# Output projection of a streaming encoder step: a block's tokens as 512 + 36 columns in place of 274 + 274

## What is computed

```python
h = rmsnorm(x, g1)
z = h @ w_in                                  # 1024 -> 8 token mixers' inputs and 3 x 1024 gates
ya, yb, yc = mlstm(z), short_conv(z), diff_attention(z)      # each (tokens, 512)
proj = jnp.einsum('btnc,ncd->btnd', br, w_br)                # each to 1024
x = x + jnp.einsum('btnd,btnd->btd', gates, proj) @ w_o      # the output projection, 1024 x 1024
h2 = rmsnorm(x, g2)
up = h2 @ w_up                                               # 1024 -> 5632
x = x + (jax.nn.silu(upc[..., :D_FF]) * upc[..., D_FF:]) @ w_dn
```

## Time and profile before

| | us |
|---|---|
| median of three runs | 1071.81 |
| lowest and highest | 1070.44, 1072.72 |
| span of the profiled execution | 1066.9 |
| TensorE busy (matmuls) | 1035.0 |
| VectorE busy | 516.5 |
| ScalarE busy | 349.4 |
| GpSimd busy | 180.8 |

### The profile page before, as it was taken

How to read it: one execution, slowest core, us unless ns; L and a number is a source line. 1 busy time by engine, 2 the same in 40 slices (tenths; PEclk the granted TensorE clock), 3 DMA queues, 4 the chain that set the end, 5 groups by cost and what they waited for, 6 DMA issues and landing times.

```text
span 1066.9 us, 19010 instructions
## 1 busy us (share of the span) xinstructions
PE 1035.0 (97%) x8074; PEld 1008.7 (95%) x8074; DVE 516.5 (48%) x712; ACT 349.4 (33%) x616; POOL 180.8 (17%) x360
## 2 busy tenths in 40 slices
PE   5999999989999999999999999999999999999996
PEld 4999899988988999999999999999999999999996
DVE  6443343323344446333334445777777777533232
ACT  5333233323344433222223333343333333322121
POOL 4001222200222212200012120112112111111010
PEclk8999999989999999999999999999999999999998
DMA  6223214371202042221513222233222232332212
GB/s 184 79 80 89 80 41 122 107 222 41 79 2 88 32 119 80 80 80 41 158 45 106 88 92 67 80 99 100 80 79 80 80 95 80 101 87 82 82 56 84
DMA packets 93451, 92.45 MB, mean 87 GB/s; under 512 B 3492, under 2 KB 86329, under 8 KB 93367
## 3 DMA queue, kind: packets, MB, share of 16 engines
q1 hardware_dynamic: 88559, 82.09, 25.2%
q10 hardware_dynamic: 3784, 6.29, 1.9%
q0 software_dynamic: 1024, 2.86, 0.9%
HBM read 86.15 MB, written 5.08 MB: 86 GB/s over the span
## 4 chain that ended last, share of the span: by engine, by line
PE 93%; DMA 2%; DVE 2%; ACT 1%; POOL 1%; issue 0%; ACTq 0%; DVEq 0%
PE D L1314 85%; DMA ck<-in_cache_k 1%; PE X L1496 1%; PE X L1532 1%; DVE hn_x L1040 1%; PE X L1466 1%; PE X L1501 1%; ACT tmp L730 0%; PE D L1399 0%; PE X L1444 0%; PE X L1443 0%; PE X L1428 0%; PE X L1446 0%; DMA x_t<-in_x_prompt 0%; PE X L1515 0%
## 5 line engine op out<-in xcount | busy, mean ns | idle before, releaser
L1314 PE MATMUL D<-h_h,w_h 128*128 128x274 f32 (+1 forms) x1744 | 367.4, 292 | 7.6 <-DVE h_l L1034 5.5
L1314 PE MATMUL D<-h_h,w_l 128*128 128x274 f32 (+1 forms) x1744 | 366.3, 291 | 0.0
L1314 PE MATMUL D<-h_l,w_h 128*128 128x274 f32 (+1 forms) x1744 | 364.6, 290 | 0.0
L984 DVE TENSOR_TENSOR w_l<-raw,w_h 128x1024 fp32r<-128x1024 f32 (+3 forms) x172 | 196.8, 1145 | 197.4 <-ACT w_h L751 192.6
L1314 PEld LDWEIGHTS D<-h_h,w_h 128*128 128x128 f32 (+1 forms) x1744 | 275.6, 189 | 10.6 <-issue 4.5
L1314 PEld LDWEIGHTS D<-h_l,w_h 128*128 128x128 f32 (+1 forms) x1744 | 276.5, 189 | 0.4
L1314 PEld LDWEIGHTS D<-h_h,w_l 128*128 128x128 f32 (+1 forms) x1744 | 276.3, 189 | 0.4
L751 ACT ACTIVATE w_h<-raw 128x1024 fp32r<-128x1024 f32 (+3 forms) x172 | 162.2, 944 | 107.7 <-PE D L1314 79.5
L952 ACT ACTIVATE acc<-ups,fcw 128x548 f32<-128x548 f32 x44 | 33.2, 755 | 168.5 <-POOL ffn_last L697 168.5
L1314 PE MATMUL D<-g_h,w_h 128*128 128x274 f32 x352 | 73.9, 291 | 0.9 <-issue 0.9
L1314 PE MATMUL D<-g_h,w_l 128*128 128x274 f32 x352 | 73.8, 291 | 0.0
(11 more groups left out here) (323 smaller groups left out, 1107.1 us busy)
## 6 DMA issues: line engine op xcount, KB each, us to landing
raw<-in_w_in SPq DMA_DIRECT2D x32, 1024.0 KB, 5.7
raw<-in_w_up SPq DMA_DIRECT2D x22, 1024.0 KB, 5.1
raw<-in_w_down SPq DMA_DIRECT2D x16, 704.0 KB, 4.5
raw<-in_w_branch SPq DMA_DIRECT2D x6, 1024.0 KB, 5.0
raw<-in_w_out SPq DMA_DIRECT2D x4, 1024.0 KB, 5.2
x_t<-in_x_prompt SPq DMA_DIRECT2D x4, 512.0 KB, 5.6
ck<-in_cache_k ACTq DMA_DIRECT2D x1, 2048.0 KB, 14.8
cv<-in_cache_v ACTq DMA_DIRECT2D x1, 2048.0 KB, 22.6
```

The lines of the kernel that those rows point to most:

```text
L984: v.tensor_tensor(lo, src, hi.bitcast(F32), ALU.subtract).then_inc(S["wl_ready"], 1)
L1314: last = t.matmul(banks(n)[0:w.shape[2], half, 0:HALF], w[:, k, :], x[:, kx, HALF * half:HALF * half + HALF], start=kx == 0 and i == 0, st ...
```

## The change

In the output projection alone the columns of a block are no longer cut in two halves of 274 but into the 512 prompt columns and the 36 others (four spare ones and the 32 sample tokens). `product` gets an argument `parts` that says where the two cuts are; all other products keep the halves. The first matmul of a pair fills a whole bank, the second 36 columns of the next one. The drain on VectorE can no longer see both banks as one pattern of equal halves, so it becomes two scalar_tensor_tensor instructions, 512 and 36 columns, of which the last one signals. The down-projection, which shares this branch, keeps one instruction.

```diff
                 elif kind in ("wo", "dn"):
 
                     dve.wait_ge(S["dense_done"], n + 1)
-                    v.scalar_tensor_tensor(out=two(xT[:, a[0], :]), in0=dbuf(n), scalar=0.5, in1=two(xT[:, a[0], :]),
-                                           op0=ALU.mult, op1=ALU.add).then_inc(S["dve_drained"], 1)
+                    if kind == "wo":
+                        for out, d in ((xT[:, a[0], 0:TP], B[:, 0, :]), (xT[:, a[0], TP:T], B[:, 1, 0:T - TP])):
+                            last = v.scalar_tensor_tensor(out=out, in0=d, scalar=0.5, in1=out, op0=ALU.mult, op1=ALU.add)
+                        last.then_inc(S["dve_drained"], 1)
+                    else:
+                        v.scalar_tensor_tensor(out=two(xT[:, a[0], :]), in0=dbuf(n), scalar=0.5,
+                                               in1=two(xT[:, a[0], :]), op0=ALU.mult, op1=ALU.add)\
+                            .then_inc(S["dve_drained"], 1)
...
-            def product(n, x_h, x_l, wait_k=None):
+            def product(n, x_h, x_l, wait_k=None, parts=((0, HALF), (HALF, T))):
...
-                            for half in range(2):
-                                last = t.matmul(banks(n)[0:w.shape[2], half, 0:HALF], w[:, k, :],
-                                                x[:, kx, HALF * half:HALF * half + HALF],
+                            for half, (c0, c1) in enumerate(parts):
+                                last = t.matmul(banks(n)[0:w.shape[2], half, 0:c1 - c0], w[:, k, :],
+                                                x[:, kx, c0:c1],
                                                 start=kx == 0 and i == 0, stop=kx == kall - 1 and i == 2)
...
                 elif kind == "wo":
-                    product(n, mg_h, mg_l, (lambda k: pe.wait_ge(S["merged_split"], k + 1)) if a[0] == 0 else None)
+                    product(n, mg_h, mg_l, (lambda k: pe.wait_ge(S["merged_split"], k + 1)) if a[0] == 0 else None,
+                            ((0, TP), (TP, T)))
```

## The result

The changed kernel takes 1086.62 us (median of four runs, 1084.81 to 1087.39), the kernel before 1071.12 us (median of four, 1070.04 to 1072.72, three of them the ones known ahead): a ratio of 1.0145, with a 95% interval of 1.013 to 1.0161, or 15.5 us more. Timed once more in a later comparison it was 1085.91 against 1069.29 us, 1.0155 (1.014 to 1.017). It is slower, and 1088.1 had been forecast, 16.3 us more.

A forecast was written before the change was run, and what follows sets the result against it. TensorE was taken to bound the kernel: 230 + 110 = 340 ns for 255.0, +85 ns a pair x 192 = +16.3 us, drain zero; 1071.8 + 16.3 = 1088.1 us, range 1084.5 to 1092.0.

The forecast's parts named there:

- The bound: Output projection: TensorE busy throughout its 48.96 us, no matmul with idle time ahead, so each added nanosecond is paid in full.
- 4.9 us around: Whole execution: the median of the runs, 1071.81 us, was put 4.9 us above the profiled span of 1066.9 us.
- When a load may start: Output projection on TensorE: a weight load starts when the matmul before its own starts; one load is ahead, not two.
- rival A: Output projection: only columns count, the short matmul costs about 30 ns; no change to +0.6 us, 1071.8 to 1072.4; chance 5%.
- The short one: 36-column matmul of each pair: priced by the distance between two loads, 110 ns, bounds 100 and 127.5 ns.
- The long one: 512-column matmul of each pair: its load uncovered, then its columns stream; 230 ns, between 219 and 238 ns.
- The drain: VectorE after each output-projection block: a second small instruction adds some 0.1 us x 8, hidden by waiting, put at zero.
- B: Output projection: a short fp32r matmul runs in two passes with one more load; 452 ns a pair, +37.8 us, chance 3%.
- C: Output projection: the clock falls to the 1.2 GHz level; 539 ns a pair, +54.5 us, 1126.3, chance 2%.
- What the profile would show: Output projection: stage 65 us instead of 49, matmul starts about 230 and 110 ns apart, 512s' loads starting with the 36s.

The follow-up runs named there:

- grouped kernel: In each output-projection block all 24 matmuls of 512 columns, then all 24 of 36, against the changed kernel's alternating pairs; 1095.14 against 1069.07 us for the kernel before, ratio 1.0245.

## Why the prediction was right, point by point

- **The bound.** TensorE in the output projection bounds the time, and a nanosecond per pair is paid in full: 16.8 us more in the stage, and the rest of the span as long as before. The absolute time was forecast from 1071.8 us, the median then known, and the four runs gave 1071.12: of the 1.5 us between 1088.1 and 1086.62, 0.7 are that and 0.8 the change. The "4.9 us around" the span set a profile of one execution against the median of others; after the change it is 1.8 us within one execution. The sum did not use it. The two-instruction drain alone changed nothing.
- **When a load may start.** Read from the pair at 590.32 and confirmed by the loads at 620.20 and 620.31. One reason given for it was not in the rows: the load path was said to lie idle before, but PEld is busy for all of the 48.96 us, its records of 190 ns overlapping at distances of 127.5. After the change there is idle time on it (57.66 us busy of 65.94), and the loads still do not start sooner; that is the evidence which the rows of before lacked. This was the step on which the sign hung; with rival A's reading nothing would have changed. The kernels with other cuts and with longer second matmuls have shown it in time as well as in records.
- **The short one.** 110 ns were taken, 108 measured. The one-column row was the right neighbour; the bound of 100 ns from the 64-column pair was read to 10 ns and lay too low, and the upper bound of 127.5 was not needed: nothing fixed comes on top.
- **The long one.** 230 ns were taken, 234 measured, inside 219 to 238. The lower end was built on 120 ns for 274 columns, a distance of two starts read to 10 ns, where the stage has 127.5. The sum was 340 ns a pair against 342, or 16.3 us against 16.8 in the stage and 15.5 to 16.6 in the runs.
- **The drain.** The small instruction costs 185 ns, and 148 ns are added to a block, near the upper bound of 159; the instruction on its own stands above it. It is hidden, as was said, by waiting time that the change made longer still.
- **Rivals.** A is excluded by the cut at 400 and by the changed kernel itself. Its 30 ns for a short matmul were the distance of two matmul records (642.85, 642.88); a record can open before its own load is done, as at 620.22, so this was no sign of a cheap first one. B (two passes) is excluded by the count: 8074 matmuls as before, 342 ns and not 452. C did not come about in the changed kernel, whose stage is at clock 1.00. But the reason given against it was weak: the grouped kernel shows that, with the same matmuls in another order, the clock falls with TensorE never idle.
- **What the profile would show.** The stage's length (65 us) and the loads that start with the 36s were as described. Wrong was the sentence on matmul starts: 230 and 110 ns were forecast, and the records have 0.32 and 0.02 us. The distances forecast are those of the loads.

## What to carry to other kernels

Where each matmul brings its own 128-column fp32r weights, at clock 1.00 as here, a moving operand under some 230 columns costs as much as 230 columns, 108 ns (36, 148 and 200 were measured): cut a row of columns into parts that are each above that, and then it doesn't matter how even they are (318 + 230 costs what 274 + 274 does, but for 1.7 us in 1070). Filling a bank to its 512 columns is no gain if a short rest is left. To price a matmul take the distance between the starts of loads in a place like it, not durations and not the starts of matmuls.

## What the runs showed of the hardware that was not expected

- The granted clock fell to half for some 3 us at a time behind runs of 24 matmuls with 36 columns each and full loads, while TensorE had no idle time (0.84 from 610 to 630 us, 0.50 from 609 to 612). It did so behind four of the eight runs. With the same matmuls put between 512s (changed kernel), with 200 columns in place of 36, and with loads of 64 columns, it stayed at 1.00 in this stage. Why the narrow loads keep it up was not tried; those runs of 24 are over in 1.36 us instead of 2.59.
- The clock also fell once behind the mean-square step in the kernel cut at 318 (0.50 from 647.71 to 651.11 us), with the instructions that the other kernels have there, whose clock stayed at 1.00. 3.40 us at half the clock are 1.7 us lost, an estimate, in which the change under study has no part.
- A matmul's record can open long before its stream: 0.02 us behind the start of the one ahead, with its own load still under way, so the record of a 512-column matmul is 0.48 us long in the changed kernel and 0.40 in the grouped one.
- A load's price goes by its columns down to 64 (57 ns for 24 in a row, against 108 for 128), also for 4-byte fp32r data.
